# Summed log decays of eight heads: a DRAM round trip and one broadcast load in place of eight selector products

## Chip, cores and metric

The kernel runs on one core of one Trainium2 chip. The metric is the device time of one execution in microseconds, the median of several runs. Before the change it is 1710.5 us (3 runs, 1710.48 to 1712.57). Engines are named as the profile names them: PE is TensorE (PEld its weight loads), DVE VectorE, ACT ScalarE, POOL GpSimd, SP the engine that issues most loads.

## What is computed

Two transformer blocks follow each other on 512 tokens of width 1024, in fp32. The first has a mixer of two halves (a chunked state-space half, SSD, with 8 heads, and an RWKV half, also with 8 heads), then a feed-forward part; the second has a three-branch mixer and a mixture of experts. The change touches only the SSD half of the first mixer. There, for each head h and each chunk of 128 tokens, with `a` the log decay of a token:

```python
a_cs = jnp.cumsum(a, axis=-1)                      # per head, within each chunk of 128
decay_in = jnp.exp(_segsum(a))                     # exp(a_cs[l] - a_cs[s]) for s <= l
scores = jnp.einsum("bclhn,bcshn->bhcls", Ch, Bh)
y_diag = jnp.einsum("bhcls,bcshp->bclhp", scores * decay_in, X)
y_off = jnp.einsum("bclhn,bchpn,bhcl->bclhp", Ch, states_in, jnp.exp(a_cs))
```

So each head needs its row `a_cs` twice with the token `l` along the free dimension and the same row on all 128 partitions: as `exp(a_cs[l])`, multiplied into `C`, and as `a_cs[l] - a_cs[s]`, where `s` is the partition.

## The kernel before, in words

The kernel is written engine by engine: each engine has one function with its instructions in order, and semaphores tie them. PSUM has eight banks; `open_` (line 466) waits until a bank was emptied, `close` signals it full, `filled` and `emptied` (lines 135 and 140) are the waits of the other engines. Weights stream through a ring of two slots (`weight_ring`, 1 MB each); SP loads a unit into a slot when its former content was used.

The stage of the change comes after the first projection. The projection runs 27 tiles on PE, which read the rounded input `x_hi`; that lies in the buffer `xn` ("normed" in the profile). ACT copies each tile out of PSUM (loop at line 1481). In between, DVE makes the step sizes `dt` and, by a scan (line 1951), the summed log decays `cs`, an 8x512 tile (`ym(5, 0, 8)`), one row per head; ACT takes two exponentials for them (lines 1489 and 1492).

Then PE does transposes, scores, the chunk states (line 716), and the loop over the heads (line 737). Before the change a head's row comes to all partitions by a product: `cs_row(h)` (line 723) multiplies an 8x128 selector (`sel16`) with `cs`, giving 128x512 in bank 5 or 6. ACT's `decay_row(h)` (line 1529) writes its exponential to `xn[:, h, :]`. DVE's `log_decays(h)` (line 2027) waits for that exponential and subtracts, out of the same bank, each partition's own sum in four instructions of 128x128 (line 2035, recorded under the helper's line 1842), into one of four buffers `s_HB`; that empties the bank. ACT takes the exponential of this buffer (line 1537). DVE multiplies the first exponential with `C` and the second with the masked scores (lines 2068 and 2069), which makes head h ready (`mt_ready`) for PE's seven small products per head (lines 743 to 755).

The order is written out by hand. On PE, `cs_row` runs two heads ahead, and behind each head comes one unit of the second block's modulation (`modulation`, line 579, 16 products straight out of a ring slot, two of them ahead of the loop). On DVE `log_decays` runs two heads ahead as well, and each head's turn ends with a piece of other work (line 2073): the preparation of the RWKV half (`prepare`, line 1958: a scan, key norms out of kk_rs, the bonus sum of line 683 of which PE computes the product), and `skipped` and `gated` for finished heads. On ACT the two preparations of line 1541 and a square root lie between the exponentials. After head 7 PE sums squares (`ssd_sums`), DVE inverts the variance (line 2080), and the RWKV half begins.

In the profile all products of PE are recorded at line 460 and transposes at line 464, ACT's activations at line 1418, DVE's helpers at 1839 (tensor-tensor), 1842 (tensor-scalar) and 1845 (scalar-tensor-tensor); instructions are told apart by shapes and tiles.

Of the kernel before, what the change touches and what calls it, by code (L numbers as in the profile page):

```python
# [6 lines left out]
F32 = mybir.dt.float32  # L7
# [3 lines left out]
ACT = mybir.ActivationFunctionType  # L11
# [3 lines left out]
T = 512  # L15
P = 128
# [62 lines left out]
def build(nc, units, fixed, x, skew, out):  # L79
    ctx = ExitStack()  # L80
    with ctx:
# [5 lines left out]
        xn = ctx.enter_context(nc.sbuf_tensor("normed", [P, KT, T], F32))  # L87
# [9 lines left out]
        def sem(name):  # L97
            if name not in sems:
                sems[name] = ctx.enter_context(nc.semaphore(name))
            return sems[name]  # L100

        def C(name, rows=P, a=0, b=None):
            o, w = CONSTS[name]
            return fix[0:rows, C0 + o + a:C0 + o + (w if b is None else b)]
# [27 lines left out]
        def bank_of(what, k=0):  # L132
            return place[what, k][0]

        def filled(eng, what, k=0, it=None):

            b, n, per = place[what, k]
            eng.wait_ge(full[b], n + 1 if it is None else it * per + (n + 1))

        def emptied(eng, what, k=0, it=None):  # L140

            b, n, per = place[what, k]
            eng.wait_ge(free[b], n + 1 if it is None else it * per + (n + 1))

        def freed(what, k=0):
            return free[place[what, k][0]]
# [93 lines left out]
        def ym(t, r0=0, r1=P):  # L240
            return A(YM + t * T, T, r0, r1)
# [196 lines left out]
        def late(n):  # L438
            at_small[0] += n
            assert at_small[0] <= C0 + CONSTS["bucket"][0] + 2 * T  # L440
            return fix[:, at_small[0] - n:at_small[0]]
# [3 lines left out]
        slot, gid_m, gid, gid_f = late(4).bitcast(I32), late(9), late(3), late(9)  # L445
        gid_i = late(9).bitcast(I32)
        rs4, rt_p, rt_e = late(4), late(64), late(16)
        slots = nc.dram_tensor("slots", (NB * P, ROW), F32, kind="Internal").ap()

        block = ctx.enter_context(nc.Block())  # L450
        PSB = [ps[:, b, :] for b in range(8)]
# [4 lines left out]
        def _(pe):  # L456
            chunk = [0]

            def mm(o, l, r, start=True, stop=True):
                return nc.tensor.matmul(o, l, r, start=start, stop=stop)  # L460
# [5 lines left out]
            def open_(what, k, b, it=None, per=0):  # L466

                if used[b]:
                    pe.wait_ge(free[b], used[b] if it is None else it * per + used[b])
                place[what, k] = (b, used[b], per)  # L470
                used[b] += 1
                return PSB[b]

            def close(last, what, k=0):
                last.then_inc(full[place[what, k][0]], 1)
# [160 lines left out]
            for t in range(NT):  # L636
                pe.wait_ge(sem(f"x{t}_loaded"), 16)
                for k in X_ORDER:
                    last = tr(PSB[bank_of("x", k)][:, t * P:(t + 1) * P], A(XT + t * D + k * P, P))
# [5 lines left out]
            for t in range(NT):  # L645
                last = mm(o[:, t * P:(t + 1) * P], x_rs[:, t:t + 1].to_broadcast([P, P]), C("ident"))
# [16 lines left out]
            for t in range(NT):  # L663
                o = open_("xs_tm", t, t)
                for k in range(4):
                    last = tr(o[:, k * P:(k + 1) * P], proj(XS + k)[:, t * P:(t + 1) * P])
# [53 lines left out]
                              A(s_XS2, 2048)[:, t * T + g * 256:t * T + (g + 1) * 256])  # L720
                close(last, "state", t)

            def cs_row(h):

                close(mm(open_("cs_row", h, 5 + h % 2), C("sel16", 8, h * P, (h + 1) * P), ym(5, 0, 8)), "cs_row", h)

            cs_row(0)
            cs_row(1)
            modulation(0)
            modulation(1)  # L730

# [4 lines left out]

            for h in range(8):
                m, e = h // 2, h % 2
                if h + 2 < 8:
                    cs_row(h + 2)  # L740
                if e == 0:
                    o = open_("ssd_y", m, m)
                pe.wait_ge(sem("mt_ready"), h + 1)
                rows = o[e * CH:(e + 1) * CH, :]
                for t in range(NT):
                    c = slice(t * P, (t + 1) * P)
                    last = mm(rows[:, c], A(s_XD, 2048)[:, t * T + h * CH:t * T + (h + 1) * CH],
                              A(s_HB + (h % 4) * T)[:, c], True, t == 0)
                    if t:
                        last = mm(rows[:, c], A(s_SI + (t - 1) * T)[:, h * CH:(h + 1) * CH],  # L750
                                  xn[:, h, c], False, True)
                if e:
                    close(last, "ssd_y", m)
                else:
                    last.then_inc(sem("ssd_head_used"), 1)
                if h == 7:
                    ssd_sums(0, 5)
                modulation(2 + h)
                if h in (1, 2):
                    prepare(0, 6 - h, 4)  # L760
# [653 lines left out]
        def _(act):  # L1414
            n_rstd = [0]

            def f(o, i, func, **kw):
                return nc.scalar.activation(o, i, func, **kw)  # L1418
# [62 lines left out]
            for t in range(N_PROJ - 1):  # L1481
                evac("proj", t, proj(t), None, ACT.Silu if ZZ <= t < ZZ + 4 else ACT.Copy)
                if 10 <= t < 18:
                    act.wait_ge(sem("conv_ready"), t - 9)
                    f(proj(XS + t - 10), proj(XS + t - 10), ACT.Silu).then_inc(sem("xbc_ready"), 1)
                if t == 18:
                    f(expA[:, :], S("a_log"), ACT.Exp)
                    act.wait_ge(sem("dt_step_ready"), 1)
                    f(ym(4, 0, 8), ym(3, 0, 8), ACT.Exp, scale=-1.0).then_inc(sem("dt_exp_ready"), 1)
                if t == 20:  # L1490
                    act.wait_ge(sem("dt_step_ready"), 2)
                    f(ym(3, 0, 8), ym(3, 0, 8), ACT.Exp).then_inc(sem("dt_exp_ready"), 1)
            act.wait_ge(sem("mixed"), 2)
            f(A(TW, T, 0, CH), proj(WA, 0, CH), ACT.Tanh).then_inc(sem("tanh_ready"), 1)
            f(proj(GL), proj(GL), ACT.Sigmoid).then_inc(sem("sigmoid_ready"), 1)
# [30 lines left out]
                i = N_MOD1 + 2 * g + j  # L1526
                evac("mod_rows", i, mod_rows2[g][j], PSB[bank_of("mod_rows", i)][:, 0:256])

            def decay_row(h):
                filled(act, "cs_row", h)  # L1530
                f(xn[:, h, :], PSB[bank_of("cs_row", h)], ACT.Exp).then_inc(sem("row_decay_ready"), 1)

            decay_row(0)
            decay_row(1)
            for h in range(8):
                emptied(act, "cs_row", h)
                f(A(s_HB + (h % 4) * T), A(s_HB + (h % 4) * T), ACT.Exp).then_inc(sem("pair_decay_ready"), 1)
                if h + 2 < 8:
                    decay_row(h + 2)
                if h == 4:  # L1540
                    prepare(0, 5)
                if h == 7:
                    rstd()
# [288 lines left out]
        def _(dve):  # L1832
# [193 lines left out]

            def log_decays(h):

                dve.wait_ge(sem("row_decay_ready"), h + 1)
                if h >= 4:  # L2030
                    head_free(h - 4)
                row = PSB[bank_of("cs_row", h)]
                for t in range(NT):
                    c = slice(t * P, (t + 1) * P)
                    last = ts(A(s_HB + (h % 4) * T)[:, c], row[:, c], d3[:, 1, t, h:h + 1], 0.0, ALU.subtract, ALU.min)
                last.then_inc(freed("cs_row", h), 1)

            def skipped(m):

# [1068 lines left out]
```

## Time and profile before

| | |
|---|---|
| median of 3 runs | 1710.5 us |
| the profiled execution's own time | 1706.67 us |
| its span | 1704.8 us |
| PE busy | 1650.2 us, 97% |
| DVE busy | 1138.8 us, 67% |
| ACT busy | 518.7 us, 30% |
| POOL busy | 682.2 us, 40% |
| mean granted clock of PE | 0.997 of full speed |

Times in a trace are counted from the start of its span. "Idle before" is the time an engine stood still ahead of an instruction, with what ended it. A granted clock of 1.00 is 2.4 GHz, 0.50 is 1.2 GHz. The page's chain is the sequence of work that ended last, followed back from the last instruction.

### The profile page before, as it was taken

The numbers are of one execution on the slowest core, as the hardware profiler recorded it, in microseconds if no ns is written. First come the engines' busy times: TensorE is split into PE (matmuls) and PEld (weight loads), VectorE is DVE, ScalarE is ACT, GpSimd is POOL, SyncE is SP. The second block draws the span as 40 slices with busy tenths as digits, with TensorE's granted clock in tenths as the row PEclk, the third lists the DMA queues.
The fourth block names the chain that finished last, engine by engine and source line by source line (L and its number), as shares of the span: only waits on it lengthen the run. The fifth ranks groups of instructions, "written<-read, shape, count | busy, mean of one in ns | idle before, by whom it ended". The sixth has DMA issues, their size and how long they took to land.

```text
span 1704.8 us, 29219 instructions
## 1 busy us (share of the span) xinstructions
PE 1650.2 (97%) x12010; PEld 1292.2 (76%) x12010; DVE 1138.8 (67%) x1543; ACT 518.7 (30%) x790; POOL 682.2 (40%) x382
## 2 busy tenths in 40 slices
PE   8999989999999999999999999999999999999998
PEld 6888567767688888888678887877878767666665
DVE  7959787756677667777774388388546526666673
ACT  4122444522231221222421132221331025544552
POOL 4765000023366666666365534345445641000000
PEclk9999999999999999999999999999999999999999
DMA  6222531131252222222222211213222256888883
GB/s 258 99 99 99 178 121 53 53 126 51 75 188 97 98 98 98 98 98 98 75 99 99 78 72 51 74 50 121 72 75 75 99 201 243 328 338 350 344 341 137
DMA packets 34070, 230.54 MB, mean 135 GB/s; under 512 B 4132, under 2 KB 4388, under 8 KB 8232
## 3 DMA queue, kind: packets, MB, share of 16 engines
q1 hardware_dynamic: 30240, 214.48, 34.6%
q10 hardware_dynamic: 2136, 10.24, 1.5%
q0 software_dynamic: 1584, 4.21, 0.8%
q8 instruction: 87, 1.43, 0.3%
q14 instruction: 23, 0.19, 0.0%
HBM read 220.98 MB, written 9.50 MB: 135 GB/s over the span
## 4 chain that ended last, share of the span: by engine, by line
PE 82%; DVE 9%; DMA 4%; ACT 2%; issue 1%; POOL 1%; SPq 0%; DVEq 0%; POOLq 0%; ACTq 0%
PE psum L460 81%; DMA arena<-units 3%; DVE arena L1839 2%; PE psum L464 1%; DVE arena L1845 1%; ACT arena L1418 1%; DVE expert_lo L1839 1%; DVE in_lo L1839 1%; ACT expert_hi L1418 1%; DVE arena L1842 1%; DVE residual L1839 0%; DVE arena L2522 0%; DMA arena<-x 0%; DVE smalls L2517 0%; DVE tiny L1853 0%
## 5 line engine op out<-in xcount | busy, mean ns | idle before, releaser
L1418 ACT ACTIVATE arena<-psum 128x512 f32<-128x512 f32 (+1 forms) x279 | 143.6, 530 | 586.2 <-PE psum L460 517.8
L1845 DVE SCALAR_TENSOR_TENSOR arena<-arena,fixed_data 128x512 f32<-128x512 f32 x138 | 197.1, 1431 | 53.1 <-ACT arena L1418 46.4
L460 PE MATMUL psum<-arena 64*64 64x64 f32 (+6 forms) x2852 | 210.6, 256 | 16.4 <-DVE arena L1839 9.0
L460 PEld LDWEIGHTS psum<-arena 64*64 64x64 f32 (+4 forms) x2852 | 140.7, 143 | 72.0 <-issue 48.8
L460 PE MATMUL psum<-normed_hi,w_in_hi 128*128 128x512 f32 x488 | 192.9, 395 | 1.1 <-ACT arena L1418 0.6
L1839 DVE TENSOR_TENSOR arena<-arena,psum 128x512 f32<-128x512 f32 (+2 forms) x200 | 112.7, 589 | 120.0 <-PE psum L460 87.6
L460 PE MATMUL psum<-normed_hi,w_in_lo 128*128 128x512 f32 x488 | 190.2, 390 | 0.0
L460 PE MATMUL psum<-in_lo,w_in_hi 128*128 128x512 f32 x488 | 190.0, 389 | 0.0
L2775 POOL TENSOR_TENSOR w_ff_lo<-weight_ring,w_ff_hi 128x1024 fp32r<-128x1024 f32 x65 | 171.7, 2642 | 5.5
L2775 POOL TENSOR_TENSOR w_in_lo<-weight_ring,w_in_hi 128x1024 fp32r<-128x1024 f32 x61 | 154.6, 2535 | 5.1
L2773 POOL TENSOR_SCALAR w_in_hi<-weight_ring 128x1024 fp32r<-128x1024 f32 x61 | 72.3, 1185 | 171.6 <-PE psum L460 155.6
L1839 DVE TENSOR_TENSOR arena<-arena 128x512 f32<-128x512 f32 (+1 forms) x135 | 131.1, 982 | 6.1 <-PE psum L460 3.8
L460 PE MATMUL psum<-normed_hi,w_ff_hi 128*128 128x512 f32 x344 | 133.9, 389 | 0.0
L460 PE MATMUL psum<-in_ff_lo,w_ff_hi 128*128 128x512 f32 x344 | 133.8, 389 | 0.0
L460 PE MATMUL psum<-normed_hi,w_ff_lo 128*128 128x512 f32 x344 | 133.8, 389 | 0.0
L2773 POOL TENSOR_SCALAR w_ff_hi<-weight_ring 128x1024 fp32r<-128x1024 f32 x65 | 70.6, 1087 | 136.4 <-PE psum L460 125.0
L2858 POOL DMA_INDIRECT out<-arena x7 | 8.7, 1245 | 270.2 <-DVE arena L1839 270.2
L460 PEld LDWEIGHTS psum<-normed_hi,w_in_hi 128*128 128x128 f32 x488 | 91.6, 188 | 23.4 <-issue 2.2
L460 PEld LDWEIGHTS psum<-in_lo,w_in_hi 128*128 128x128 f32 x488 | 91.6, 188 | 19.4
L460 PEld LDWEIGHTS psum<-normed_hi,w_in_lo 128*128 128x128 f32 x488 | 91.6, 188 | 18.9 <-issue 0.5
L2773 POOL TENSOR_SCALAR w_br_hi<-weight_ring 128x1024 fp32r<-128x1024 f32 x41 | 46.2, 1127 | 149.1 <-PE psum L460 149.1
L2831 POOL TENSOR_SCALAR w_out_hi<-weight_ring 128x1024 fp32r<-128x1024 f32 x8 | 10.7, 1332 | 237.2 <-PE psum L460 237.2
(299 smaller groups left out, 3570.8 us busy)
## 6 DMA issues: line engine op xcount, KB each, us to landing
weight_ring<-units SPq DMA_DIRECT2D x124, 1024.0 KB, 4.9
arena<-units SPq DMA_DIRECT2D x55, 1024.0 KB, 7.8
normed<-units SPq DMA_DIRECT2D x20, 1024.0 KB, 8.4
slots<-arena ACTq DMA_DIRECT2D x7, 516.0 KB, 8.9
arena<-slots SPq DMA_DIRECT2D x7, 516.0 KB, 5.8
fixed_data<-fixed ACTq DMA_DIRECT2D x1, 2944.0 KB, 10.3
arena<-x SPq DMA_DIRECT2D x4, 512.0 KB, 5.9
arena<-bias_rows ACTq DMA_DIRECT2D x2, 896.0 KB, 4.3
```

What stands on the lines that cost most here:

```text
L460: return nc.tensor.matmul(o, l, r, start=start, stop=stop)
L464: return nc.tensor.transpose(o, i, C("ident", k, 0, k))
L1418: return nc.scalar.activation(o, i, func, **kw)
L1839: return V.tensor_tensor(o, a, b, op)
L1842: return V.tensor_scalar(o, a, s1, s2, op0) if op1 is None else V.tensor_scalar(o, a, s1, s2, op0, op1)
L1845: return V.scalar_tensor_tensor(o, a, s1, b, op0, op1)
L2773: first = nc.gpsimd.tensor_scalar(hi, raw, 1.0, 1.0, ALU.mult, ALU.mult)
L2775: nc.gpsimd.tensor_tensor(lo, raw, hi.bitcast(F32), ALU.subtract).then_inc(sem("split_ready"), 1)
L2831: ch.link(nc.gpsimd.tensor_scalar(hi, raw, 1.0, 1.0, ALU.mult, ALU.mult))
L2858: nc.gpsimd.indirect_dma_start(out[:, :], bass.IndirectOffsetOnAxis(ap=xb[b % 3][:, D + 4:D + 5].bitcast(I32), axis=0), xb[b % 3][:, 0:D], ...
```

## The change

PE's eight `cs_row` products go, and with them ACT's reads of their banks. Instead ACT, right after the wait for the summed log decays, issues a store of the 8x512 tile `cs` to a DRAM tensor `decays` (16 KB). After its last copy of the projection it waits for that store and issues one load that reads the 16 KB once for each partition (a step of 0 over 128 partitions) and fills all of `xn` (128 x 4096 fp32, 2 MB). DVE's `log_decays` waits for this load instead of ACT's exponential and reads `xn` instead of PSUM. ACT then takes the exponential of `xn[:, h, :]` in place, behind DVE's subtractions for that head, followed by the exponential of the differences.

```diff
--- before.py
+++ after.py
@@ -445,6 +445,7 @@
         slot, gid_m, gid, gid_f = late(4).bitcast(I32), late(9), late(3), late(9)
         gid_i = late(9).bitcast(I32)
         rs4, rt_p, rt_e = late(4), late(64), late(16)
+        decays = nc.dram_tensor("decays", (8, T), F32, kind="Internal").ap()
         slots = nc.dram_tensor("slots", (NB * P, ROW), F32, kind="Internal").ap()
 
         block = ctx.enter_context(nc.Block())
@@ -720,12 +721,6 @@
                               A(s_XS2, 2048)[:, t * T + g * 256:t * T + (g + 1) * 256])
                 close(last, "state", t)
 
-            def cs_row(h):
-
-                close(mm(open_("cs_row", h, 5 + h % 2), C("sel16", 8, h * P, (h + 1) * P), ym(5, 0, 8)), "cs_row", h)
-
-            cs_row(0)
-            cs_row(1)
             modulation(0)
             modulation(1)
 
@@ -736,8 +731,6 @@
 
             for h in range(8):
                 m, e = h // 2, h % 2
-                if h + 2 < 8:
-                    cs_row(h + 2)
                 if e == 0:
                     o = open_("ssd_y", m, m)
                 pe.wait_ge(sem("mt_ready"), h + 1)
@@ -1489,7 +1482,11 @@
                     f(ym(4, 0, 8), ym(3, 0, 8), ACT.Exp, scale=-1.0).then_inc(sem("dt_exp_ready"), 1)
                 if t == 20:
                     act.wait_ge(sem("dt_step_ready"), 2)
+                    act.dma_start(decays, ym(5, 0, 8)).then_inc(sem("decays_stored"), 16)
                     f(ym(3, 0, 8), ym(3, 0, 8), ACT.Exp).then_inc(sem("dt_exp_ready"), 1)
+            act.wait_ge(sem("decays_stored"), 16)
+            rows = bass.AP(tensor=decays.tensor, offset=decays.offset, ap=[[0, P], [1, 8 * T]])
+            act.dma_start(xn.rearrange("p h n -> p (h n)"), rows).then_inc(sem("decay_rows_loaded"), 16)
             act.wait_ge(sem("mixed"), 2)
             f(A(TW, T, 0, CH), proj(WA, 0, CH), ACT.Tanh).then_inc(sem("tanh_ready"), 1)
             f(proj(GL), proj(GL), ACT.Sigmoid).then_inc(sem("sigmoid_ready"), 1)
@@ -1526,17 +1523,10 @@
                 i = N_MOD1 + 2 * g + j
                 evac("mod_rows", i, mod_rows2[g][j], PSB[bank_of("mod_rows", i)][:, 0:256])
 
-            def decay_row(h):
-                filled(act, "cs_row", h)
-                f(xn[:, h, :], PSB[bank_of("cs_row", h)], ACT.Exp).then_inc(sem("row_decay_ready"), 1)
-
-            decay_row(0)
-            decay_row(1)
             for h in range(8):
-                emptied(act, "cs_row", h)
+                act.wait_ge(sem("log_decays_ready"), h + 1)
+                f(xn[:, h, :], xn[:, h, :], ACT.Exp)
                 f(A(s_HB + (h % 4) * T), A(s_HB + (h % 4) * T), ACT.Exp).then_inc(sem("pair_decay_ready"), 1)
-                if h + 2 < 8:
-                    decay_row(h + 2)
                 if h == 4:
                     prepare(0, 5)
                 if h == 7:
@@ -2026,14 +2016,14 @@
 
             def log_decays(h):
 
-                dve.wait_ge(sem("row_decay_ready"), h + 1)
+                dve.wait_ge(sem("decay_rows_loaded"), 16)
                 if h >= 4:
                     head_free(h - 4)
-                row = PSB[bank_of("cs_row", h)]
+                row = xn[:, h, :]
                 for t in range(NT):
                     c = slice(t * P, (t + 1) * P)
                     last = ts(A(s_HB + (h % 4) * T)[:, c], row[:, c], d3[:, 1, t, h:h + 1], 0.0, ALU.subtract, ALU.min)
-                last.then_inc(freed("cs_row", h), 1)
+                last.then_inc(sem("log_decays_ready"), 1)
 
             def skipped(m):
```

## Rows read from the trace of the kernel before

**Rows 1.** The page's chain that ended last, shares of the span by engine.

```profile
...
PE 82%; DVE 9%; DMA 4%; ACT 2%; issue 1%; POOL 1%; SPq 0%; DVEq 0%; POOLq 0%; ACTq 0%
```

**Rows 2.** Chain in order of time, 180 to 236: start us, us, what.

```profile
...
183.57 4.86 DMA weight_ring<-units
...
200.15 0.61 ACT normed L1418
...
215.90 2.36 PE psum L460 x30
```

**Rows 3.** DVE's groups by form, 182.72 to 217.2: busy us, mean ns, idle before, releasers.

```profile
...
L1842 DVE TENSOR_SCALAR arena<-psum,smalls 128x128 f32<-128x128 f32 x32 | 8.9, 345 | 4.7 <-ACT normed L1418 4.5
```

**Rows 4.** DVE's timeline, 160 to 219: start us, us, line, operation, tiles, shapes, count.

```profile
...
182.74 2.16 DVE L1842 TENSOR_SCALAR arena<-psum,smalls 128x128 f32<-128x128 f32 x8
184.82 0.68 DVE L1839 TENSOR_TENSOR normed<-arena,normed 128x512 f32<-128x512 f32 x1
...
186.09 1.13 DVE L1842 TENSOR_SCALAR arena<-psum,smalls 128x128 f32<-128x128 f32 x4
...
189.12 0.69 DVE L1839 TENSOR_TENSOR arena<-arena 128x512 f32<-128x512 f32 x1
...
192.30 1.22 DVE L1972 TENSOR_TENSOR_SCAN arena<-fixed_data,arena 128x512 f32<-128x512 f32 x1
...
197.04 0.68 DVE L1839 TENSOR_TENSOR arena<-arena,psum 128x512 f32<-128x512 f32 x1
...
215.16 2.02 DVE L1839 TENSOR_TENSOR arena<-arena 128x512 f32<-128x512 f32 x3
```

**Rows 5.** PE's timeline, 180 to 202.6, the same columns.

```profile
...
180.53 1.98 PE L460 MATMUL psum<-arena,fixed_data 8*128 8x512 f32 x4
182.44 1.94 PE L460 MATMUL psum<-weight_ring,tiny 128*32 128x256 f32 x32
...
190.52 0.65 PE L460 MATMUL psum<-arena 128*64 128x128 f32 x4
...
192.19 1.07 PE L460 MATMUL psum<-weight_ring,tiny 128*32 128x256 f32 x16
193.19 1.09 PE L460 MATMUL psum<-fixed_data,smalls 128*64 128x128 f32 x16
...
197.94 2.18 PE L460 MATMUL psum<-arena,fixed_data 128*128 128x512 f32 x4
```

**Rows 6.** All tensor-scalar instructions (line 1842) by operands: ns min/median/max.

```profile
...
L1842 DVE TENSOR_SCALAR fixed_data<-fixed_data,smalls x16: 289/486/2210, 1188.1 to 1280.6; 128x128 f32<-128x128 f32 x4, 128x256 f32<-128x256 f32 x4, 128x384 f32<-128x384 f32 x4, 128x512 f32<-128x512 f32 x4
```

**Rows 7.** Stretches: length, busy PE, PEld, DVE, ACT, POOL, granted clock, DMA share, GB/s.

```profile
...
167.50:182.50 15.00, 14.66 (x91) 10.78 (x94) 11.23 (x20) 10.12 (x15) 0.00 (x0) 1.00 0.00 0
182.50:217.20 34.70, 30.47 (x285) 18.52 (x285) 29.71 (x65) 10.88 (x18) 0.00 (x0) 1.00 0.71 247
226.00:231.00 5.00, 5.00 (x82) 4.29 (x85) 4.61 (x10) 2.39 (x4) 0.00 (x0) 0.66 0.01 3
```

**Rows 8.** PE's timeline behind the loop: the idle time before, and its releaser, in brackets.

```profile
...
226.00 0.69 PE L460 MATMUL psum<-arena 64*64 64x64 f32 x32 [3.41 <-DVE arena L1845]
```

**Rows 9.** ACT's timeline, 150 to 219.

```profile
...
151.30 0.63 ACT L1418 ACTIVATE arena<-arena 8x512 f32<-8x512 f32 x1 [16.77 <-DVE arena L1839]
...
166.86 0.60 ACT L1418 ACTIVATE arena<-psum 128x512 f32<-128x512 f32 x1 [4.84 <-PE psum L460]
```

**Rows 10.** DMA issues by line: count, KB each, median us from issue to landing.

```profile
...
fixed_data<-fixed ACTq DMA_DIRECT2D x1, 2944.0 KB, 10.3
...
arena<-bias_rows ACTq DMA_DIRECT2D x2, 896.0 KB, 4.3
fixed_data<-fixed ACTq DMA_DIRECT2D x1, 1288.0 KB, 13.7
```

**Rows 11.** ACT's timeline at the kernel's start, a DMA issue on its queue.

```profile
...
10.93 0.34 ACTq L1469 DMA_DIRECT2D fixed_data<-fixed  x1
```

**Rows 12.** Loads of weight_ring issued from 183 to 222.

```profile
...
DMA to landing us min/median/max: 4.6/4.9/6.4
```

## The prediction

> **What bounds the kernel now.** I read the page's chain first: TensorE (PE) has 82% of it [rows 1], so a change elsewhere pays only where the chain leaves PE. Next the chain in order of time, around the loop over the eight heads: there it hops from a weight load (4.86 us) over PE to ScalarE's exponential out of PSUM, to VectorE (DVE) and back to PE [rows 2]. No engine is the bound alone; the round PE, ACT, DVE is: PE's selector product puts a head's summed log decays on all partitions, ACT takes their exponential, DVE subtracts. Third, DVE's groups in this loop: 32 subtractions (line 2035) of 345 ns each, and before them 4.7 us of idle time, 4.5 of it put down to ACT's exponential of the row [rows 3]. Fourth, DVE's timeline: the first multiply of head 0 starts at 184.82, the multiply that makes head 7 ready is the first of the three that start at 215.16 and so ends near 215.86 [rows 4]. The loop's length for DVE is 215.86 - 184.82 = 31.04 us. After that multiply PE needs 2.36 us to the sums on which DVE goes on [rows 2], so what head 7's multiply gains, the kernel gains.
>
> **The change, part by part.**
>
> *Eight products leave PE.* Two stand ahead of the loop (1.98 us from 180.53, the modulations following at 182.44), six inside at some 1.1 us each [rows 5]. The modulation products behind the first two start 1.9 us earlier, so the first weight slot comes free earlier and the 4.86 us load that head 0's modulation waited for is in time. This alone moves no DVE instruction; it is counted at nothing by itself.
>
> *DVE no longer waits for rows.* All rows are in SBUF before the loop, if the transfer lands in time (below), so the 4.7 us of idle before the subtractions go [rows 3].
>
> *The subtractions read SBUF instead of PSUM.* Nearest row: tensor-scalar, SBUF to SBUF, 128x128, a scalar per partition: 289 ns at least [rows 6], against 345: 56 ns less. Four took 1.13 us [rows 4], that is (1.13 - 0.345) / 3 = 0.26 from start to start; with 0.056 less four need about 0.91 (0.82 to the next start), a gain of 0.22 a head. Six heads count, 1.3 us; the first two lie ahead of 184.82, where ACT's two exponentials set the start, which stays. Bounds: 0 (if issue sets the pace) and 0.3 a head. The same row's maximum, 2210 ns, is what GpSimd at work beside them can do; it has 0.00 us here [rows 7], so this is not charged. The Trainium skill (VectorE: DVE Perf Modes, the section on the TRN2 errata) gives 120 + FD cycles for fp32 from PSUM and 58 + FD/2 from SBUF, at 0.96 GHz: an estimate of 131 ns less per instruction. By that page the six heads gain 3.1 us and not 1.3, and the sum below could be up to 0.9 better; the measured rows decide for 1.3.
>
> *What is late next.* Without the round, DVE and PE meet at the bonus sum: DVE's step after its fourth multiply pair needs PE's 2.18 us product. From head 1's readiness PE does two heads (1.67 each), two modulations (1.00 each), kk_rs (1.03) and the bonus [rows 5]: 1.67 + 1.00 + 1.03 + 1.67 + 1.00 + 2.18 = 8.55. DVE from the same point does three groups of subtractions (0.82 each), the scan (1.22, some 1.13 to the next start), two pairs of multiplies (186.09 - 184.82 = 1.27 each) and two linked multiplies (0.68 each, 1.44 with the links) [rows 4]: 2.46 + 1.13 + 2.54 + 1.44 = 7.6. New wait: 8.55 - 7.6, about 1.0. The loop becomes 31.04 - 4.7 - 1.3 + 1.0 = 26.0, **5.0 us less**.
>
> *PE's clock.* Ahead of head 0 PE now ends its two modulations at about 182.5 and waits for DVE until 186.1: 3.6 us idle, where a product stood before, and then head 0. The trace has such a gap: 3.41 us idle up to 226.00 [rows 8], and behind it a granted clock of 0.66 over 226 to 231 [rows 7], a stretch at 1.2 GHz between stretches at 2.4. It cost PE 5 x 0.34 = 1.7 us. The same after 186 would delay heads 0 and 1 and modulations on PE by up to 1.7; PE has 0.6 of slack there (its modulation done near 189.0; head 1's second multiply, 0.69 from 189.12 [rows 4], less 0.22, ready at 189.6), part of the slow stretch may fall in idle time, and the rest feeds the bonus wait: 0.4 to 1.1, I take 0.8. The Trainium skill (TensorE: Matmul & The Clock Gate, Part 1) states that the slow state is the default and only activity lifts it, which speaks against taking work from PE; the trace agrees with [rows 7, 8], and without that rule the sum would be 4.9.
>
> *Store and load on ACT's queue.* The store of 16 KB is issued at about 151.3 ahead of an exponential [rows 9] whose reader on DVE (line 1956) stands three mixing steps further on; the copies behind it on ACT run into 4.84 of idle before 166.86 [rows 9]: nothing. ACT waits for it again only behind the last projection, 15 us later; the transfers of [rows 10] carry 56 to 184 times the bytes in 4.3 to 13.7 us, so that wait is over at arrival, and tanh, sigmoid and all of ACT's preparation queued behind it don't stand. The load is issued beside the copy at 166.86 (0.60 us) [rows 9]; an issue took 0.34 [rows 11], which the copy covers if the two run side by side and lays open if not. Cost 0.1, bounds 0 and 0.5, on the path since tanh follows. SP's and GpSimd's queues are not passed.
>
> *The load's landing.* 2 MB. Row for 1 MB: 4.86, twice that 9.7 [rows 2]; for 2944 KB 10.3, so 7.2 [rows 10]; 896 KB read like this from a few KB of DRAM: 4.3, so 9.8 [rows 10]. Issued at 167.0 it lands at 174 to 177; the DMA engines moved 0 GB/s from 167.5 to 182.5 [rows 7], so nothing collides. DVE, with all heads queued behind, asks for it at 182.74 [rows 4]. Cover: 5 to 8 us; it costs nothing now, and each microsecond beyond 15.7 of flight costs one.
>
> **Sum:** 5.0 - 0.8 - 0.1 = 4.1 us. The profiled execution took 1706.67 (span 1704.8), 3.8 under the median of 1710.5; it would go to 1702.6, and the median to **1706.4**. Nothing behind the loop keeps a schedule of its own: loads follow PE's and GpSimd's steps, so the shift is carried to the end. About 0.2% (3.4 us) is what a measurement of this kernel can tell from no change.
>
> **Rivals.**
> - *The clock holds.* The new gap doesn't pull the clock down: 4.9, 1705.6. If the one behind 226 goes too, since everything moves against it, another 1.7: 1703.9. For it: the gap at 226 alone shows the fall [rows 7, 8]. Against: the new gap is as long.
> - *Weight loads pace the heads.* With two slots, two heads can't be closer than a landing plus a modulation. At the median landing of 4.9 that is 6.0 against DVE's 6.9; at the longest, 6.4 [rows 12], it is 7.5, some 0.3 a head over seven heads, 2 us: saving 2, 1708.4. A subtraction that gains nothing from SBUF leads near there too.
> - *The rows land late (slower).* All 128 partitions read the same 16 KB. The slowest row, 1288 KB in 13.7 [rows 10], would make 21.8: landing at 188.8, 6.1 late, against 4.9 gained (no clock loss counted): 1.2 slower, 1711.7. It costs from 15.7 us of flight, and is slower by over 0.2% from about 24, below 90 GB/s. Against it: the 896 KB rows, read from even less DRAM, moved at 208 GB/s.
> - *The change does not free DVE*: DVE stays tied to ACT's exponential, now by a wait for both of a head's exponentials. Two heads are subtracted ahead, so 3.4 us cover 1.2; excluded, no price.
>
> **How the numbers follow.** Forecast 0.42; clock holds 0.20; loads pace or SBUF gives nothing 0.28; rows late 0.10. Faster: nearly all of the first two and little of the third, 0.60; slower: two thirds of the late rows, 0.07; same: 0.33. The range runs from both gaps without a fall (1703.9) to nearly no gain: 1703.8 to 1709.8.
>
> **What would show it.** Right: eight products of shape 8x512 with 128-partition output gone; the load landing before 178; subtractions near 290 ns without idle time before them; DVE's idle in the loop near 1 us, before the bonus multiply; a low clock just behind 186; head 7's multiply ending near 211.7. Wrong: DVE idle behind the load at 182.7; PE waiting for weight_ring in several heads; the subtractions at 345 ns; or the loop shorter and the 4.1 lost again behind it.

## The result, and the profile after

The changed kernel took 1703.38 us (median of 6 runs, 1701.23 to 1705.98) against 1712.44 (6 runs) for the kernel before: a ratio of 0.9946, 95% interval 0.9933 to 0.996. Two more comparisons of the same two kernels, told below, gave 0.9967 (0.9944 to 0.9991) and 0.9964 (0.9939 to 0.9988). So it is faster, as forecast, and by more than forecast: 4.1 us were expected, and 1703.38 lies 0.4 below the range.

The profiled execution took 1703.58 us (span 1701.6). Its chain by engine, from the page: DMA has gone from 4% to 3% and PE from 82% to 80%, DVE from 9% to 12% [rows 1].

```profile
PE 80%; DVE 12%; DMA 3%; ACT 3%; issue 1%; POOL 1%; SPq 0%; DVEq 0%; POOLq 0%; ACTq 0%
```

DVE's groups by form, 182.9 to 211.7 us, as [rows 3]:

```profile
...
L1832 DVE TENSOR_SCALAR arena<-normed,smalls 128x128 f32<-128x128 f32 x32 | 6.9, 280 | 0.0
...
L1829 DVE TENSOR_TENSOR arena<-arena,psum 128x512 f32<-128x512 f32 x3 | 2.1, 688 | 1.0 <-PE psum L461 1.0
```

The 32 subtractions are at 280 ns instead of 345, and the 4.7 us of idle before them are 0.0. One wait of 1.0 us is new, for PE. DVE's timeline, as [rows 4]:

```profile
...
182.99 1.66 DVE L1832 TENSOR_SCALAR arena<-normed,smalls 128x128 f32<-128x128 f32 x8
185.08 0.69 DVE L1829 TENSOR_TENSOR normed<-arena,normed 128x512 f32<-128x512 f32 x1 [0.43 <-ACT arena L1411]
...
186.29 0.87 DVE L1832 TENSOR_SCALAR arena<-normed,smalls 128x128 f32<-128x128 f32 x4
...
194.59 0.69 DVE L1829 TENSOR_TENSOR arena<-arena,psum 128x512 f32<-128x512 f32 x1 [0.95 <-PE psum L461]
...
198.16 0.69 DVE L1829 TENSOR_TENSOR arena<-arena,psum 128x512 f32<-128x512 f32 x1
...
209.90 2.01 DVE L1829 TENSOR_TENSOR arena<-arena 128x512 f32<-128x512 f32 x3
...
```

Head 0's first multiply starts at 185.08, and head 7 is ready near 210.60, the end of the first of the three multiplies from 209.90. The loop is 25.52 us, against 31.04 before: **5.5 us less**. PE's timeline, as [rows 5, 8]:

```profile
...
180.77 1.94 PE L461 MATMUL psum<-weight_ring,tiny 128*32 128x256 f32 x32
186.52 0.85 PE L461 MATMUL psum<-arena 128*64 128x128 f32 x4 [3.81 <-DVE arena L1829]
...
193.45 1.09 PE L461 MATMUL psum<-fixed_data,smalls 128*64 128x128 f32 x16
...
196.99 1.13 PE L461 MATMUL psum<-arena,fixed_data 128*128 128x512 f32 x2
...
220.74 1.04 PE L461 MATMUL psum<-arena 64*64 64x64 f32 x32 [3.41 <-DVE arena L1835]
```

The gap ahead of head 0 is there (3.81 us), the old one of 3.41 as well. The bonus sum of line 683 takes 1.13 us, in 2 instructions; this row matters most below. The new wait is not one for the bonus sum: that product starts at 196.99 only, and DVE's step with the wait starts at 194.59, when the kk_rs product (193.45, 1.09 us) has just ended. DVE's step that reads the bonus sum is the one at 198.16, with some 0.1 us of idle time ahead of it. Stretches, with the columns of [rows 7]:

```profile
...
167.50:182.50 15.00, 14.66 (x119) 11.25 (x118) 11.24 (x21) 9.77 (x15) 0.00 (x0) 1.00 0.34 140
...
186.00:190.00 4.00, 3.48 (x22) 2.96 (x26) 3.96 (x11) 1.23 (x3) 0.00 (x0) 0.60 0.63 262
...
220.00:225.00 5.00, 4.26 (x54) 4.01 (x58) 4.38 (x9) 1.67 (x3) 0.00 (x0) 0.66 0.01 3
...
```

Behind either gap the granted clock falls (0.60 and 0.66: most of the stretch at 1.2 GHz, where 1.00 is 2.4). ACT's timeline and its queue, as [rows 9]:

```profile
...
151.57 0.54 ACTq L1485 DMA_DIRECT2D decays<-arena  x1
152.16 0.63 ACT L1411 ACTIVATE arena<-arena 8x512 f32<-8x512 f32 x1 [17.35 <-DVE arena L1829]
...
167.11 0.60 ACT L1411 ACTIVATE arena<-psum 128x512 f32<-128x512 f32 x1 [4.84 <-PE psum L461]
167.12 0.36 ACTq L1489 DMA_DIRECT2D normed<-decays  x1
167.60 0.62 ACT L1411 ACTIVATE arena<-arena 64x512 f32<-64x512 f32 x1
...
```

The load's issue ran beside the copy, and tanh follows at 167.60. The page gives the load's landing, in its DMA issues:

```profile
normed<-decays ACTq DMA_DIRECT2D x1, 2048.0 KB, 6.8
```

It lands near 174.0, 9 us ahead of its first reader at 182.99.

**Where the rest of the time came from.** I matched DVE's instructions of several executions one by one, and give how much later (or, with a minus, earlier) each stood than in the first execution of the kernel before. The loop starts with the first multiply of head 0. The columns 290, 1376 and 1669 are instructions that stood there, in us.

| execution | loop starts | head 7 | 290 | 1376 | 1669 | loop alone | from loop's start to 290 |
|---|---|---|---|---|---|---|---|
| before, first | 0 | 0 | 0 | 0 | 0 | 0 | 0 |
| before, second | 0.1 | 0.0 | -0.8 | -0.2 | 3.2 | 0.0 | -0.8 |
| before, third | 1.3 | 1.6 | 2.1 | 2.0 | 3.3 | 0.3 | 0.8 |
| after, first | 0.3 | -5.3 | -6.2 | -6.4 | -3.2 | -5.5 | -6.5 |
| after, second | 1.6 | -3.9 | -4.9 | -2.7 | 2.2 | -5.5 | -6.5 |
| after, third | 1.7 | -3.8 | -4.3 | -4.8 | -3.4 | -5.5 | -6.0 |

The loop gains 5.5 us in each of the three, and by 290 us the mean is 6.3. What lies outside differs between executions of the same kernel by as much as the gain: the three of before are up to 3.3 us apart at the end, the three of after 5.6.

### The profile page after: what moved, and what is told of

The parts are those of the page before. It is cut to its first block, busy times and chain, and to the rows that moved or that the text cites. A ratio compares the mean times of both kernels' runs of the same rounds, so it can differ in the third digit from the quotient of the medians.

```text
span 1701.6 us, 29189 instructions
## 1 busy us (share of the span) xinstructions
PE 1645.1 (97%) x11994; PEld 1292.8 (76%) x11994; DVE 1135.0 (67%) x1543; ACT 517.7 (30%) x790; POOL 685.3 (40%) x382
## 4 chain that ended last, share of the span: by engine, by line
PE 80%; DVE 12%; DMA 3%; ACT 3%; issue 1%; POOL 1%; SPq 0%; DVEq 0%; POOLq 0%; ACTq 0%
PE psum L461 79%; DVE arena L1829 4%; DMA arena<-units 3%; DVE arena L1835 2%; ACT arena L1411 1%; PE psum L465 1%; DVE arena L1832 1%; DVE in_lo L1829 1%; DVE expert_lo L1829 1%; DVE residual L1829 0%; ACT expert_hi L1411 0%; DVE arena L2512 0%; DMA arena<-x 0%; DVE smalls L2507 0%; DVE tiny L1843 0%
## 5 line engine op out<-in xcount | busy, mean ns | idle before, releaser
L1829 DVE TENSOR_TENSOR expert_lo<-arena,expert_hi 128x2048 fp32r<-128x2048 f32 x36 | 82.1, 2291 | 37.5 <-ACT expert_hi L1411 37.5
```

Of the source, the lines that this page charges most:

```text
L1829: return V.tensor_tensor(o, a, b, op)
```

## The experiments

Where a loop's start, head 7 or a later instruction is given with a small signed number, it counts as in the table above.

**Both kernels again**, unedited, the first two with five rounds of timing in one comparison.

> The kernel before once more, with a profile of its own. Both theories: ratio 1.000. Theory A: its span is 3 to 6 us longer than the 1704.8 of the first profile, the difference lies behind 1376 us, in the expert stage, and a stretch of low clock stands there (as in the profile of the changed kernel from 1422 on). Theory B: its span is near 1705 again, with no such stretch.

> The changed kernel unchanged, timed beside the kernel before in five rounds. Theory A (the freed loop gives some 6 us, the first profile of the kernel before was short in its expert stage): ratio 0.9963, 6.4 us less, and the first multiply of head 7 about 5.3 us earlier than before. Theory B (the change itself is worth the 9 us of the first comparison, so 3 us more come from somewhere behind the loop): ratio 0.9947.

Measured: before 1712.18 (ratio 1.0013, 0.9992 to 1.0034), after 1705.05 (0.9967, 0.9944 to 0.9991) beside 1711.86 of before. The gain is 6.8 us here, not 9.1. The profiled execution of before came out as Theory A has it: its span is 1708.0 us, 3.2 longer than the first, the difference lies behind 1376 us (table above), and a stretch at a low clock stands there:

```profile
...
1422.00:1434.00 12.00, 8.84 (x32) 6.93 (x31) 9.66 (x14) 6.60 (x6) 0.85 (x1) 0.78 0.63 233
...
```

> The kernel before, one more look. Theory: its expert stage is some 3 us longer than in the first profiled execution, as it was in the second one, with a stretch at the lower clock of about 6.8 us near 1428 us. Rival: the first execution's shorter expert stage is the usual one.

> The changed kernel, unedited, once more. The traces of before and after, matched instruction by instruction, account for 6.4 us like for like; the first timed comparison gave 9.1 us and the second 7. Theory: the true difference is 6 to 7 us (ratio 0.9957 to 0.9967), and what the first comparison had beyond it is scatter of the runs in the expert stage. Rival: a part of the gain that no profiled execution shows, then the ratio comes out near 0.9946 again (9 us).

Measured, in a third comparison: after 1705.37 beside 1711.75, 6.4 us, ratio 0.9964 (0.9939 to 0.9988). The median lies in the theory's 6 to 7 us; the interval, 2 to 10 us, takes in the rival's 0.9946 as well. All runs of the three comparisons and of one more that shared the kernel before, together: 26 of after have a median of 1704.44, 92 of before 1711.92, 7.5 us apart. The third execution of before came out otherwise than expected: its end is 3.3 us later than in the first, but 2.0 of that were there already at 1376 us, and the clock near 1428 did not fall. Its stretches there, and at 178, where PE has no idle time at all:

```profile
...
178.00:182.00 4.00, 4.00 (x12) 3.08 (x10) 1.55 (x3) 0.07 (x1) 0.00 (x0) 0.57 0.00 0
1422.00:1434.00 12.00, 8.97 (x47) 7.34 (x47) 9.03 (x18) 7.67 (x8) 2.74 (x3) 1.00 0.78 303
...
```

**psum_sub**: was the tie ACT's exponential? The products stay and DVE still subtracts out of PSUM, but waits for PE alone; ACT takes the row exponentials from the loaded rows.

```diff
-            def decay_row(h):
-                filled(act, "cs_row", h)
-                f(xn[:, h, :], PSB[bank_of("cs_row", h)], ACT.Exp).then_inc(sem("row_decay_ready"), 1)
...
             for h in range(8):
                 emptied(act, "cs_row", h)
+                f(xn[:, h, :], xn[:, h, :], ACT.Exp)
...
-                dve.wait_ge(sem("row_decay_ready"), h + 1)
+                filled(dve, "cs_row", h)
```

> The eight products stay and DVE subtracts out of PSUM as before; only ACT's exponentials take their rows from the load, so DVE waits for PE alone and not for ACT's read of the bank. Theory A (the round over ACT was the cost, PE's products second): PE then paces the heads at 1.67 + 1.00 + 1.1 = 3.8 us a head, head 7's multiply ends near 212.5: 3 to 3.5 us less than before, ratio 0.998. Rival C (the products leaving PE is what pays): nothing gained, ratio 1.000. Rival D (ACT's round alone is all): the full gain, 0.9963.

Measured: 1711.4 us, ratio 0.9999 (0.998 to 1.0017). Head 7 stands where it stood before (the three multiplies start at 215.17). DVE's group of subtractions, 182.72 to 217.2, and one row of DVE's timeline:

```profile
...
L1841 DVE TENSOR_SCALAR arena<-psum,smalls 128x128 f32<-128x128 f32 x32 | 8.9, 344 | 4.6 <-PE psum L461 4.3
```

```profile
...
191.89 1.12 DVE L1841 TENSOR_SCALAR arena<-psum,smalls 128x128 f32<-128x128 f32 x4 [1.94 <-PE psum L461]
...
```

The same idle time as in [rows 3], now put down to PE. ACT's exponential had only been the last of two to come; the product that it reads, which stands in PE's order behind a head and a modulation, ended hardly sooner. So the round of the prediction had the right engines and the wrong tie. This execution also had a low clock where the first execution of before has 1.00 [rows 7]:

```profile
...
186.00:190.00 4.00, 3.52 (x22) 3.00 (x26) 3.92 (x9) 1.19 (x3) 0.00 (x0) 0.58 1.01 426
...
```

From head 0 to head 1 PE took 5.30 us (186.48 to 191.78) against 4.27 before (186.25 to 190.52). By an estimate from these rows, taking ACT out of the wait is worth up to about 1 us at a full clock, not the 3 to 3.5 expected; the timed interval reaches 3 us to either side and does not settle it.

**transfers_only**: the kernel before with the store and the load added, ACT's first row exponential waiting for the load since it writes the same buffer.

```diff
+            act.dma_start(decays, ym(5, 0, 8)).then_inc(sem("decays_stored"), 16)
...
+            act.dma_start(xn.rearrange("p h n -> p (h n)"), rows).then_inc(sem("decay_rows_loaded"), 16)
...
+            act.wait_ge(sem("decay_rows_loaded"), 16)
             decay_row(0)
```

> The kernel before with the store and the 2 MB load added, products and all else as before (ACT waits for the load ahead of its first row and overwrites it). Theory A (the transfers are free): ratio 1.000, the load lands 7 us after its issue. Rival E (the issue on ACT's queue or the traffic costs): 0.3 to 0.5 us or more at tanh, ratio 1.0003 and up.

Measured: 1711.85 us, ratio 1.0009 (0.9985 to 1.0032). The transfers cost nothing that can be measured; the interval alone would leave room for up to 5 us. The loop is narrower: 31.42 us (185.98 to 217.40), against 31.36 in the third execution of before, which had the same low clock at 178 us (0.57, here 0.59).

**products_idle**: the changed kernel, with the eight products put back in PE's order, into banks that nobody reads.

```diff
+            def idle_row(h):
+                b = 5 + h % 2
+                pe.wait_ge(free[b], used[b])
+                mm(PSB[b], C("sel16", 8, h * P, (h + 1) * P), ym(5, 0, 8))
+            idle_row(0)
+            idle_row(1)
             modulation(0)
...
+                if h + 2 < 8:
+                    idle_row(h + 2)
```

> The changed kernel with the eight products put back on PE at their old places, into banks that nobody reads. Theory A2 (before the change DVE waited for a product that stood in PE's order behind a head and a modulation; it is the tie that cost, and PE's time for the products comes second): PE then needs some 3.8 us a head and reaches DVE again through kk_rs and the bonus sum; head 7's multiply ends 2 to 4 us before that of the kernel before, instead of 5.3. Rival C (PE's time for the products is all of the gain): it ends where it did before, no gain. Rival D (the products cost nothing, only the tie did): 5.3 us earlier as in the changed kernel.

Measured: 1709.64 us, ratio 0.9991 (0.9966 to 1.0017); the interval reaches from no gain to that of the changed kernel in its second comparison (0.9967), so the trace has to tell. Its loop starts 1.0 later and head 7 is 2.0 earlier: it takes 27.99 us (185.84 to 213.83), 3.05 less than before, where the changed kernel has 5.5. DVE's groups, 182.72 to 214, and rows of its timeline:

```profile
...
L1842 DVE TENSOR_SCALAR arena<-normed,smalls 128x128 f32<-128x128 f32 x32 | 6.9, 280 | 0.0
...
L1839 DVE TENSOR_TENSOR arena<-arena,psum 128x512 f32<-128x512 f32 x3 | 2.1, 688 | 3.5 <-PE psum L461 3.5
...
```

```profile
...
196.62 0.69 DVE L1839 TENSOR_TENSOR arena<-arena,psum 128x512 f32<-128x512 f32 x1 [2.22 <-PE psum L461]
...
201.39 0.69 DVE L1839 TENSOR_TENSOR arena<-arena,psum 128x512 f32<-128x512 f32 x1 [1.24 <-PE psum L461]
...
217.51 0.29 DVE L1851 TENSOR_SCALAR tiny<-psum 128x128 f32<-128x128 f32 x1 [2.37 <-PE psum L461]
...
```

The subtractions wait for nothing, and DVE waits for PE all the same, at the next steps that read PE's sums (kk_rs, then the bonus): 3.5 us instead of 4.7. These 1.2 and six heads of quicker subtractions at 1.13 - 0.87 = 0.26 [rows 4], 1.6, make 2.8 of the 3.05. Behind head 7 PE is late once more: DVE waits 2.37 us for the sums ahead of the variance, 1.11 before and in the changed kernel. So by 290 us only 1.9 us are left, counted from the loop's start, of the 6.0 to 6.5 of the changed kernel; neither all of the gain (Rival C) nor nothing (Rival D) goes with PE's time for the products.

Not all of these 4.1 to 4.6 us is the products' doing. This execution had a low clock ahead of the loop, as some others have (last section):

```profile
...
178.00:182.00 4.00, 4.00 (x14) 3.00 (x14) 2.06 (x3) 0.53 (x2) 0.00 (x0) 0.70 0.00 0
...
```

PE begins its modulations 2.0 us later than before (184.49 for 182.44) and DVE its loop 1.0 later, so PE enters the loop 1.0 further behind. Without that, by this estimate, PE's time for the products is worth 3.1 to 3.6 us at 290 us, about half of the gain; the rest is the quicker subtractions and the tie that is gone.

**warm_gap**: the changed kernel with ten throwaway products of 128x128 in the gap ahead of head 0.

```diff
                     o = open_("ssd_y", m, m)
+                if h == 0:
+                    warm(10, 5)
                 pe.wait_ge(sem("mt_ready"), h + 1)
```

> The changed kernel with ten throwaway 128x128 products on PE in its idle time ahead of head 0 (after the two modulations). Theory A2: no low clock behind 186, the 0.95 us that DVE waited at the bonus sum falls to near 0 since the bonus product takes 1.13 us; head 7's multiply ends 0.5 to 1.0 us earlier than in the changed kernel, time 0.5 to 1.0 us less. Rival F (the low clock there costs nothing, DVE waits for the bonus anyway): head 7's multiply ends where it does in the changed kernel.

Measured: 1704.19 us, ratio 0.9951 (0.9931 to 0.9972). The loop starts at 0.2 and head 7 stands at -6.3: a loop 6.5 us shorter. PE's timeline, the stretch behind 186, and DVE's group that reads PE's sums (182.72 to 214):

```profile
...
182.60 2.50 PE L461 MATMUL psum<-fixed_data 128*128 128x128 f32 x20
186.39 0.65 PE L461 MATMUL psum<-arena 128*64 128x128 f32 x4 [1.29 <-DVE arena L1831]
...
```

```profile
...
186.00:190.00 4.00, 3.05 (x32) 2.15 (x33) 3.96 (x11) 1.20 (x3) 0.00 (x0) 1.00 0.63 262
...
```

```profile
...
L1831 DVE TENSOR_TENSOR arena<-arena,psum 128x512 f32<-128x512 f32 x3 | 2.1, 687 | 0.1
...
```

With the gap filled the clock stays at 1.00 behind it, and DVE's wait for kk_rs is gone; the 0.1 that is left of the group's 1.0 stands at the bonus sum. So the fall costs 1.0 us, and that wait is the fall, not a wait of its own. This is shown for the loop; the timed ratio is not apart from that of the changed kernel, and in the profiled execution 2.2 us were lost again near 311 us (-6.8 at 290 us, -4.6 at 390), where the clock was 0.87 over 309 to 315.

**late_load**: the changed kernel with the load issued only behind ACT's preparation of the chunks, 10.7 us later.

```diff
-            act.wait_ge(sem("decays_stored"), 16)
-            rows = bass.AP(tensor=decays.tensor, offset=decays.offset, ap=[[0, P], [1, 8 * T]])
-            act.dma_start(xn.rearrange("p h n -> p (h n)"), rows).then_inc(sem("decay_rows_loaded"), 16)
...
             evac("chunk_decay", 0, c_last[:, :], PSB[bank_of("chunk_decay")][:, 0:32], ACT.Exp)
+            act.wait_ge(sem("decays_stored"), 16)
+            rows = bass.AP(tensor=decays.tensor, offset=decays.offset, ap=[[0, P], [1, 8 * T]])
+            act.dma_start(xn.rearrange("p h n -> p (h n)"), rows).then_inc(sem("decay_rows_loaded"), 16)
```

> The changed kernel with the load issued 11 us later, behind ACT's copy of the chunk decays (about 178.3). It lands near 185.1 if the flight stays 6.8 us. Theory A2: DVE stands still from 183.0 until then, 2.1 us, and the whole of it is carried to head 7 and to the end: time 2 us more than the changed kernel. Rival G (the wait is made up behind, at the bonus sum or in PE's slack): less than 1 us more.

Measured: 1707.1 us, ratio 0.9962 (0.9944 to 0.998). The load was issued at 177.79 and took 7.3 us. DVE's timeline:

```profile
...
185.15 1.66 DVE L1832 TENSOR_SCALAR arena<-normed,smalls 128x128 f32<-128x128 f32 x8 [2.51 <-DMA normed<-decays]
...
```

Head 7 is ready 2.6 us later than in the changed kernel (-2.7 for -5.3). Of that, 2.16 are the late landing (185.15 for 182.99), which is carried whole, as the rival of the late rows had it. The other 0.45 are a longer wait for kk_rs (1.40 for 0.95): PE stands 6.29 us ahead of head 0 instead of 3.81, and the low clock behind it lasts longer (0.70 over 190 to 195 us, where the changed kernel has 0.98). The timed ratio is not apart from that of the changed kernel; only the trace shows the price.

**skip_early** and **warm_skip**: the gap of 3.41 us behind the loop ends with a `skipped` piece on DVE. In the first it is moved ahead of the inversion of the variance; the second is the first with warm_gap's products.

```diff
                 if h == 7:
+                    skipped(3)
                     invert_variance("sum_ssd0", 1.0 / 256, 1e-6)
...
                 masked_gram("abT", m, r_Z, k_level[0])
-                if m == 0:
-                    skipped(3)
```

> The changed kernel with DVE's skip step of the last pair of heads (its read of PSUM bank 3) taken before the variance of the first group instead of behind the first masked products. Theory A2 (behind the loop DVE sets the pace; PE stands 3.41 us because bank 3 is emptied late): PE's idle time of 3.41 falls below 1.5, DVE's 1.1 us ahead of the variance is filled with the step, and no or less low clock follows: 1 to 3 us less than the changed kernel. Rival H (DVE's work behind the loop is the bound whatever its order): less than 0.7 us.

> The changed kernel with both single edits together: ten throwaway products of 128x128 in the gap before head 0, and DVE's last `skipped` piece moved ahead of the inversion of the variance. If the fall of the clock behind 186 and the 3.41 us gap behind the loop each cost what the two single runs showed (1.0 and about 1.1 us), the traces should show neither low stretch, head 7's multiply ending 6.3 us earlier than in the kernel before, and the wait of 3.41 us gone, some 8 us in all at 290 us. Time by that: about 1.5 to 2 us under the changed kernel's. Rival: TensorE's clock falls are moved and not removed (a stretch at the lower level turns up elsewhere), and the time equals the changed kernel's within 1 us.

Measured: skip_early 1704.54 us, ratio 0.9962 (0.9941 to 0.9983); warm_skip 1703.07, 0.996 (0.9932 to 0.9989), in the comparison that had 1705.37 and 0.9964 for the changed kernel. In skip_early the longest of PE's waits between 208 and 240 is this one, in place of 3.41:

```profile
...
PE psum L465 <- DVE arena L1835: 1.5, 1, 1.5
...
```

The clock behind it fell all the same, against the expectation:

```profile
...
221.00:226.00 5.00, 4.33 (x60) 3.35 (x61) 4.93 (x11) 2.39 (x4) 0.00 (x0) 0.66 0.02 3
...
```

From the loop's start to 290 us skip_early gained 1.4 - (-6.2) = 7.6 us and warm_skip 1.6 - (-7.0) = 8.6, where the changed kernel had 6.0 to 6.5. In warm_skip both low stretches are gone, but another turned up, at 311 us:

```profile
...
186.00:190.00 4.00, 2.63 (x25) 2.19 (x27) 3.58 (x9) 2.54 (x5) 0.00 (x0) 1.00 0.99 414
...
221.00:226.00 5.00, 3.76 (x104) 2.99 (x105) 4.90 (x9) 1.59 (x4) 0.00 (x0) 1.00 0.00 0
309.00:315.00 6.00, 5.14 (x98) 3.60 (x102) 3.00 (x7) 2.26 (x4) 0.00 (x0) 0.72 0.06 10
...
```

DVE's instruction that was 7.0 earlier at 290 gives way to one 4.6 earlier at 390, so 2.4 were lost there in this execution; the second execution of the changed kernel lost 2.2 at the same place, the other two nothing. Both executions with throwaway products lost some 2 us there, so the rival, that the falls are moved and not removed, is not excluded. warm_skip has the lowest median of all, but its interval takes in that of the changed kernel: that it beats it is shown in the trace up to 290 us, not in the time.

## Why the prediction was right in direction and short in size

**What bounds the kernel.** That a gain at head 7 is a gain of the kernel held: in the first execution of after the 5.5 us of the loop were still there at 1376 us (6.4). It holds as long as PE is not behind: in products_idle it is, and 1.3 us of head 7's gain are lost on the way to the sums. The round was read one step off: ACT's exponential was named as the tie from its 4.5 us in [rows 3], and psum_sub, which takes it out, gained nothing, or by the estimate above 1 us at most.

**The eight products** were "counted at nothing by itself". That step failed in its weight. Put back with nobody reading them, they leave 3.05 us of the loop's gain and 1.9 of 6.0 to 6.5 at 290 us, about 1.0 of the loss being, by the estimate above, the low clock of that execution. The sum as a whole did not suffer, since the wait that they cause was counted on DVE's side, with the 4.7.

**The subtractions.** 345 to 280 ns, 0.26 a head against 0.22, 1.6 us for 1.3; the nearest row, 289 [rows 6], was a good stand-in. The Trainium skill (VectorE: DVE Perf Modes, the section on the TRN2 errata) gave an estimate of 131 ns less; the measured 65 ns do not bear it out, and the measurement decides.

**What is late next** is the step that failed and made the forecast short: a term of the sum that was mis-sized. It took "PE's 2.18 us product" from a row marked x4 [rows 5] as the bonus sum, and so put a new wait of 1.0 us into the sum. That row held the bonus sum and a selector product merged; after shows the bonus alone, x2, at 1.13. With 1.13 the working reads 8.55 - 1.05 = 7.5 on PE against 7.6 on DVE: no new wait, and warm_gap, where the clock does not fall, measured 0.1. A wait of 1.0 us came all the same, for another reason (the clock) and nearly all of it one step earlier, at kk_rs: that the sign "DVE's idle in the loop near 1 us" came true is luck.

**The clock.** Forecast at 0.8 behind a new gap; it fell where forecast, and warm_gap puts it at 1.0. Because PE and DVE meet so closely, at kk_rs and again at the bonus sum, this 1.0 is just what shows as DVE's new wait. The prediction thus charged 1.0 and 0.8 for what is 1.0 in all. With that and the 0.3 of the subtractions its loop comes to 4.2 + 0.8 + 0.3 = 5.3, where 5.5 was measured.

**Store, load and landing.** Right: transfers_only finds no cost; the issue hid behind the copy (the 0.1 was not there: DVE stands 0.3 later already at 34 us, long before it); 6.8 us of flight against 7.2 to 9.8. The rival of late rows did not come about, and late_load shows that it would have cost what it said, and some of the clock on top.

**The other rivals.** The clock did not hold. Weight loads do not pace the heads: the timeline of PE has one wait of 1.00 us for a load in the loop, at 206.83. The fall behind the old gap stayed, as forecast.

**Behind the loop** 0.5 to 1.0 us more were gained up to 290 us in each execution of after, measured from head 7; the three executions of before differ by 1.3 there, so no cause is settled. The traces account for 6.3 us, the timed runs for 6.4, 6.8 and 9.1. The intervals of all three ratios take in 6.8 to 9.6 us, but what put the first at 9.1 stays open: no profiled execution shows a place for it. The forecast's own base was low too: 1710.5 came from three runs, where 92 have 1711.92.

## What to carry to other kernels

Before a merged timeline row serves as a duration, split it by its count: an "x4" where one product is "x2" is two products, and here that one row was worth a microsecond in a sum of five. Idle time is put down to the last that came; ask what stands in the queue ahead of it, since taking away the last alone may gain little. A sign that comes true in size may come from another cause; look which instruction waits. Moving rows to all partitions by a small store and one wide load cost nothing here as long as the load landed ahead of its first reader, and past that point the delay was paid in full.

## What the runs showed of the hardware that was not expected

- The granted clock falls at different places in different executions of one kernel. At 178 to 182 us PE was busy for all of the 4 us, as in the 4 us ahead of them, and the clock was at 0.57 in the third execution of before and at 1.00 in the first [rows 7]; of after, the first has 1.00, the second 0.62 and the third 0.57. The stretch of 1422 to 1434 was at 0.72 in the first execution of after, and at 1.00, 0.78 and 1.00 in the three of before; the one near 311 us comes and goes too. Which execution gets them was not settled; they hide effects of 2 us, which is why the loop was read against its own start. The Trainium skill (TensorE: Matmul & The Clock Gate, Part 1) states, of a kernel's start, that the number of products that run at the lower level differs from run to run of one kernel; these rows show the like in a kernel's middle.
- Ten throwaway products, 2.5 us of PE, kept the clock at 1.00 behind the gap, where it had been 0.60.
- A load that reads 16 KB of DRAM once for each of 128 partitions moved 2 MB in 6.8 us, some 300 GB/s, more than the 208 GB/s of the nearest row [rows 10].
